# Halved column sums, attention operands split inside the projection, and modulation slots issued earlier, in a six-layer transformer kernel

## The chip, the cores and the metric

The kernel runs on one core of a Trainium2 chip, as one program and one launch. The metric is the device time of one execution in microseconds. TensorE (PE) multiplies matrices, VectorE (DVE), ScalarE (ACT) and GpSimd (POOL) work on rows of 128 partitions, and SyncE (SP) issues the DMA transfers.

## The reference

Two blocks run one after the other on 512 tokens of width 1024. The first has two hybrid layers; each mixes causal attention over selected keys, a gated linear attention and a pooling over token windows, and then applies a gated feed-forward network with a short convolution. The second has four layers on the same tokens laid out as a grid of 64 by 8, with 256 context tokens beside them; the kind of attention turns with the layer (0: grouped queries, 1: a neighbourhood window, 2: the difference of two maps, then 0 again).

```
h  = rms_norm(x, norm_g[i]) * (1 + sc) + sh        # sc, sh, gt = silu(c) @ ada_w[i] + ada_b[i]
hc = rms_norm(xc, norm_g[i]) * (1 + scc) + shc
u, z = split(h @ w_in);  uc, zc = split(hc @ w_in)
q, k = axial_rope(rms_norm(q, q_g)), axial_rope(rms_norm(k, k_g))       # kinds 0 and 2
o  = attention(q, [kc, k], [vc, v])                # kind 2: p0 - lam * p1, then a norm
lam = exp(sum(lq1 * lk1)) - exp(sum(lq2 * lk2)) + lambda_init
x  = x + gt * ((o * silu(z)) @ w_out)
```

`ada_w` is 1024 by 3072 for every one of the four layers; its products (the modulation) are worked out during the first block. Between the blocks x is normed once more (`final_norm_g`), and the first norm of the second block needs the sum of squares of every token again.

## The kernel before, in words

x lies in SBUF with the width on partitions: eight chunks k of 128 by the tokens (`M.xT[:, k, :]`). Every large product is made in float32 from two float32r parts: ACT rounds a weight slot of 128 by 1024 to its high part (L139, `split_high`), POOL subtracts to get the low part (L147, `split_low`), and PE multiplies high by high, high by low and low by high (L166). The two buffers of split slots are `M.head`, which stays for the whole program, and `WS`, which each stage takes anew; `M.W` is a ring of four slots loaded by DMA (L111).

The program is a sequence of stages (`stage`, L76 to L86). In a stage each engine has its own written order and waits on semaphores; at the end of each all engines meet. Nothing is scheduled by a planner. The stages that the change touches:

- `start`: x is loaded, ACT squares the chunks (L451), PE adds each chunk over the partitions with four matmuls against a column of ones (`column_sums`, L234), ACT takes the root (L241) and PE spreads it (L249). Then the first weight slot is split by ACT and POOL.
- `attention_by_keys` in the first block (16 works x of 128 queries; PE goes through scores L1104, transposes L1538, products L1553 and L1557). Beside it run the side programs of `MixedIn`: modulation products (L883, `slots`) whose weights go through the same ring `M.W`, their turning into columns (L898), and the two products of the pooled tokens (L1021), which DVE takes (L1043).
- `gated_linear_attention`: PE's order is written out by hand and holds `slots(a, b)` (24 weight slots of the modulation) and `columns(a, b)` between the steps of the attention. At the end DVE stores the modulation (L904), ACT and POOL split the first slot of the next stage into `M.head` (L154, L159), and SP waits for the slots loaded ahead (L115).
- `between_blocks`: DVE norms chunk k and turns its tokens into grid order (L314) into one of two buffers, ACT squares it (L286) and copies it back to `M.xT` (L287); PE adds 8 chunks of 512 tokens and 8 of 256 context tokens (L234).
- `values_projection` and `tiles_projection` in each second-block layer: 18 tiles t in a layer of kind 0, 24 in the others. For kind 0 tiles 0 to 7 are queries, 8 and 9 keys, 10 to 17 the gate z. Roots of the norms are taken at tile `z_tile + 2` (L2235, L2269), spread by PE (L2201) and applied by DVE (L2277).
- `first_rows`: a stage of its own, in which ACT rounds the first pair of heads (L1069, L1083), DVE and POOL make the low parts (L1072, L1086), and PE runs three idle products (`keep_running`, L175). For kind 1 it also loads the band of biases and adds the window (L1096), for kind 2 it works out lam (L2315 to L2329).
- `attention_by_keys` (kinds 0 and 1) or `difference_attention` (kind 2).

## Time and profile before

| | |
|---|---|
| time, median of 3 runs | 3480.87 us (3474.05 to 3481.51) |
| the profiled execution | 3467.25 us, span 3465.5 us |
| PE busy | 93% of the span |
| DVE, ACT, POOL busy | 43%, 39%, 33% |
| DMA | 260.00 MB, mean 75 GB/s |

The span is the time from the first to the last instruction in the profile; the time of the execution is 1.75 us more. Busy shares are averages over stages that have different limits. Where PE stands still its idle time is shown in square brackets behind the next instruction, with what ended it. PEclk is the clock that was granted to TensorE as a share of 2.4 GHz; 0.50 is 1.2 GHz. A matmul of float32 operands shows as two instructions in the trace.

### The profile page before, as it was taken

The numbers are of one execution on the slowest core, as the hardware profiler recorded it, in microseconds if no ns is written. First come the engines' busy times: TensorE is split into PE (matmuls) and PEld (weight loads), VectorE is DVE, ScalarE is ACT, GpSimd is POOL, SyncE is SP. The second block draws the span as 40 slices with busy tenths as digits, with TensorE's granted clock in tenths as the row PEclk, the third lists the DMA queues.
The fourth block names the chain that finished last, engine by engine and source line by source line (L and its number), as shares of the span: only waits on it lengthen the run. The fifth ranks groups of instructions, "written<-read, shape, count | busy, mean of one in ns | idle before, by whom it ended". The sixth has DMA issues, their size and how long they took to land. (4 is left out here: it accounts for less than half of the span.)

```text
span 3465.5 us, 52212 instructions
## 1 busy us (share of the span) xinstructions
PE 3223.5 (93%) x20824; PEld 2623.2 (76%) x20824; DVE 1503.8 (43%) x2673; ACT 1341.1 (39%) x2457; POOL 1143.7 (33%) x628
## 2 busy tenths in 40 slices
PE   7988999999989999989999999978999987799999
PEld 6856788777667887888787888767878766688687
DVE  4973443117744432132376310257323348733373
ACT  3352333223433332243366312257232236724463
POOL 3531444345414443424101322233234311225202
PEclk9999999999989999989999999999999999899999
DMA  4344222223442222212000111110112200013102
GB/s 142 113 168 168 81 96 92 88 86 119 166 175 79 93 96 88 97 59 89 26 2 20 55 56 61 55 41 14 49 62 85 80 20 1 1 50 105 47 2 74
DMA packets 80664, 260.00 MB, mean 75 GB/s; under 512 B 11808, under 2 KB 13600, under 8 KB 80416
## 3 DMA queue, kind: packets, MB, share of 16 engines
q1 hardware_dynamic: 80416, 256.58, 22.2%
q8 instruction: 169, 2.77, 0.3%
q14 instruction: 79, 0.65, 0.1%
HBM read 239.24 MB, written 2.10 MB: 70 GB/s over the span
## 5 line engine op out<-in xcount | busy, mean ns | idle before, releaser
L166 PE MATMUL ps<-hs,head 128*128 128x512 f32 x4176 | 882.3, 368 | 18.2 <-PEq L86 5.9
L166 PE MATMUL ps<-hs,WS 128*128 128x512 f32 x4176 | 869.3, 366 | 5.5 <-POOL WS L147 5.5
L166 PEld LDWEIGHTS ps<-hs,head 128*128 128x128 f32 x4176 | 717.1, 190 | 176.3 <-issue 19.4
L166 PEld LDWEIGHTS ps<-hs,WS 128*128 128x128 f32 x4176 | 714.2, 189 | 149.1 <-issue 9.1
L147 POOL TENSOR_TENSOR WS<-W,WS 128x1024 fp32r<-128x1024 f32 x168 | 408.7, 2433 | 637.9 <-ACT WS L139 637.9
L147 POOL TENSOR_TENSOR head<-W,head 128x1024 fp32r<-128x1024 f32 x165 | 399.1, 2419 | 653.0 <-ACT head L139 653.0
L139 ACT CAST WS<-W 128x1024 fp32r<-128x1024 f32 x168 | 175.9, 1047 | 360.0 <-PE ps L166 330.0
L1571 ACT ACTIVATE prob<-ps,low 128x768 f32<-128x768 f32 (+4 forms) x320 | 223.2, 699 | 192.2 <-DVE low L1643 189.9
L1104 PE MATMUL ps<-kk,qq 64*128 64x256 f32 (+3 forms) x2064 | 221.3, 342 | 71.9 <-ACT prob L1308 34.7
L1104 PEld LDWEIGHTS ps<-kk,qq 64*128 64x128 f32 x2064 | 163.8, 192 | 140.1 <-issue 73.9
L139 ACT CAST head<-W 128x1024 fp32r<-128x1024 f32 x165 | 172.8, 1047 | 214.6 <-PE ps L166 211.2
L1643 DVE TENSOR_REDUCE low<-ps 128x1 f32<-128x768 f32 (+4 forms) x320 | 216.5, 701 | 57.9 <-PE ps L1104 53.5
L1076 POOL TENSOR_TENSOR qq<-prj,qq 128x512 fp32r<-128x512 f32 (+1 forms) x52 | 53.1, 1022 | 455.8 <-ACT qq L1069 455.8
L1538 PE MATMUL ps<-const,prob 128*128 128x128 f32 x1312 | 185.0, 284 | 15.3 <-ACT probT L1579 13.0
L1975 DVE TENSOR_TENSOR glu<-cg,glu 128x512 fp32r<-128x512 f32 x44 | 81.1, 1843 | 270.7 <-ACT glu L1962 270.7
L1553 PE MATMUL ps<-probT,vtok 128*64 128x128 f32 x2624 | 179.2, 279 | 2.4 <-DVE prj L1627 2.4
L1538 PEld LDWEIGHTS ps<-const,prob 128*128 128x128 f32 x1312 | 143.7, 143 | 43.6 <-ACT prob L1571 22.5
L2239 ACT ACTIVATE prj<-ps,par 128x768 f32<-128x768 f32 (+1 forms) x52 | 45.2, 869 | 313.7 <-PE ps L166 313.7
L1553 PEld LDWEIGHTS ps<-probT,vtok 128*64 128x64 f32 x2624 | 140.6, 137 | 27.5 <-issue 27.3
L166 PE MATMUL ps<-glu,head 128*128 128x512 f32 x528 | 131.5, 406 | 11.7 <-PEq L86 11.7
L1579 ACT COPY probT<-ps 128x512 f32<-128x512 f32 (+3 forms) x272 | 139.4, 540 | 1.8 <-PE ps L1538 1.5
L2001 DVE TENSOR_TENSOR xT<-xT,ps 128x512 f32<-128x512 f32 x32 | 22.0, 687 | 269.3 <-PE ps L166 269.3
(283 smaller groups left out, 3924.7 us busy)
## 6 DMA issues: line engine op xcount, KB each, us to landing
W<-in_stream_dram SPq DMA_DIRECT2D x432, 512.0 KB, 3.5
swap<-prj SPq DMA_DIRECT2D x168, 64.0 KB, 2.4
band<-in_bias_band_dram SPq DMA_DIRECT2D x8, 512.0 KB, 3.4
prj<-prj SPq DMA_DIRECT2D x64, 64.0 KB, 3.0
xT<-in_x_dram SPq DMA_DIRECT2D x4, 512.0 KB, 8.4
W<-in_stream_dram SPq DMA_DIRECT2D x1, 2048.0 KB, 13.4
out_dram<-xT SPq DMA_DIRECT2D x8, 256.0 KB, 2.7
xT<-in_ctx_dram SPq DMA_DIRECT2D x1, 1024.0 KB, 6.0
```

What stands on the lines that cost most here:

```text
L139: nc.scalar.copy(WS[j % 2][:, 0, :], M.W[:, (pos + j) % RING, :]).then_inc(high, 1)
L147: nc.gpsimd.tensor_tensor(WS[j % 2][:, 1, :], M.W[:, (pos + j) % RING, :], WS[j % 2][:, 0, :], ALU.subtract).then_inc(split, 1)
L166: last = pe.matmul(out, a(i), b(j), start=start and n == 0, stop=stop and n == 2)
L1076: return self.nc.gpsimd.tensor_tensor(self.q_part(s, 1, cols), self.queries(t, cols), self.q_part(s, 0, cols), ALU.subtract)
L1104: last = pe.matmul(out(hd)[:, sc:sc + c], self.qq[half(hd), s, i, q0:q0 + P], self.kk[half(hd), s_keys, j, kc:kc + c], start=n == 0, stop= ...
L1538: last = pe.transpose(turn_at(y, hd, j), prob[:, (2 * y + hd) % 4, sc:sc + P], M.const[:, C_ID:C_ID + P])
L1553: pe.matmul(summed_at(hd), M.vtok[:, kb, v_col(p) + 64 * hd:v_col(p) + 64 * hd + 64], probT[:, (2 * y + hd) % 4, j, :], start=j == 0, stop ...
L1571: nc.scalar.activation(prob[:, u % 4, c0:c0 + n], W.scores(M, x, hd)[:, c0:c0 + n], ACT.Exp, bias=low[:, u:u + 1], accum_out=total[:, u:u ...
L1579: nc.scalar.copy(probT[:, u % 4, 0:n, :], M.ps[:, 4 + 2 * hd, 0:n * P].rearrange("p (x n) -> p x n", n=P)).then_inc(turn_copied, 1)
L1643: nc.vector.tensor_reduce(low[:, u:u + 1], W.scores(M, x, hd)[:, c0:c0 + n], AX_X, ALU.max, negate=True).then_inc(maxed, 1)
L1975: nc.vector.tensor_tensor(glu[:, 1, f - 2, :], g[:, f % 2, :], glu[:, 0, f - 2, :], ALU.subtract).then_inc(glu_split, 1)
L2239: nc.scalar.activation(M.prj[:, t, 0:n], flat(bank(t), n), ACT.Copy, scale=gain(t)).then_inc(evicted, 1)
```

## The change

It has these parts, named A to G below.

**A, between the blocks.** `turned` and `squares` hold all eight chunks. The copy back to `M.xT` is a DMA for each chunk, issued by SP, and no longer done by ACT. POOL adds the squares of each two chunks, and PE adds over the partitions only the four sums of pairs, and four of the context.

```diff
+                    sp.wait_ge(scaled, k + 1)
+                    sp.dma_start(M.xT[:, k, 0:S], turned[:, k, :]).then_inc(moved, 16)
                 sp.wait_ge(pars_loaded, 32)
+                sp.wait_ge(moved, 16 * KD)
...
-                    if k >= 2:
-                        act.wait_ge(added, k - 1)
-                    nc.scalar.activation(squares[:, k % 2, :], turned[:, k % 2, :], ACT.Square).then_inc(squared, 1)
-                    nc.scalar.copy(M.xT[:, k, 0:S], turned[:, k % 2, :]).then_inc(moved, 1)
...
+                    for c in range(2 * (k - 3), 2 * (k - 2)) if 3 <= k < 7 else ():
+                        nc.scalar.activation(ctx_squares[:, c, :], M.xT[:, c, S:N], ACT.Square
+                                             ).then_inc(ctx_squared, 1)
+                act.wait_ge(added, 1)
...
+                def pair(x, k, done, summed):
+                    pool.wait_ge(done, k + 2)
+                    nc.gpsimd.tensor_tensor(x[:, k, :], x[:, k, :], x[:, k + 1, :], ALU.add).then_inc(summed, 1)
+
+                for k in range(0, KD, 2):
+                    pair(squares, k, squared, paired)
+                    if k >= 4:
+                        pair(ctx_squares, 2 * k - 8, ctx_squared, ctx_paired)
+                        pair(ctx_squares, 2 * k - 6, ctx_squared, ctx_paired)
...
+                for i in range(KD // 2):
+                    pe.wait_ge(paired, i + 1)
+                    last = column_sums(pe, M, squares[:, 2 * i, :], 0, i == 0, i == KD // 2 - 1)
+                    for c in range(2 * (i - 2), 2 * (i - 1)) if i >= 2 else ():
+                        pe.wait_ge(ctx_paired, c + 1)
+                        last = column_sums(pe, M, ctx_squares[:, 2 * c, :], QT, c == 0, c == KD // 2 - 1)
+                last.then_inc(added, 1)
```

**B, the opening stage.** POOL adds chunks 4 and 5, and 6 and 7; PE adds six blocks where it added eight. A root of one column is taken ahead, so that the table of the square root is loaded earlier.

```diff
-                for k in range(KD):
+                for k in range(KD // 2):
                     pe.wait_ge(squared, k + 1)
-                    last = column_sums(pe, M, squares[:, k, :], 0, k == 0, k == KD - 1)
+                    column_sums(pe, M, squares[:, k, :], 0, k == 0, False)
+                for i, k in enumerate(range(KD // 2, KD, 2)):
+                    pe.wait_ge(paired, i + 1)
+                    last = column_sums(pe, M, squares[:, k, :], 0, False, k == KD - 2)
...
+                for k in range(KD // 2, KD, 2):
+                    pool.wait_ge(squared, k + 2)
+                    nc.gpsimd.tensor_tensor(squares[:, k, :], squares[:, k, :], squares[:, k + 1, :], ALU.add
+                                            ).then_inc(paired, 1)
...
                 nc.scalar.activation(M.cos[:], M.cos[:], ACT.Sin)
                 act.wait_ge(eps_set, 1)
+                nc.scalar.activation(M.rstd[:, QT:QT + 1], M.eps[:], ACT.Sqrt)
                 act.wait_ge(summed, 1)
                 column_root(nc, M, S).then_inc(rooted, 1)
```

**C, the causal attention.** The product of the pooled tokens is issued right behind the scores of its work, and DVE takes it in the same round; the fifth group of columns is turned at work 13. **E** (last lines): in the attention of the second block, kinds 0 and 1, PE runs four idle products behind the scores of works 0 and 1.

```diff
-    TURN_AT = {5: 0, 7: 1, 9: 2, 11: 3, 16: 4, 17: 5}
+    TURN_AT = {5: 0, 7: 1, 9: 2, 11: 3, 13: 4, 17: 5}
...
+    def mix(self, pe, x):
+
...
-        if x - 1 in self.MIX_AT:
-            i = self.MIX_AT[x - 1]
+        if x in self.MIX_AT:
+            i = self.MIX_AT[x]
             dve.wait_ge(self.mixed, i + 1)
...
+                        if x < 2 and not side:
+                            keep_running(pe, M, 4, 7)
+                    if side:
+                        side.mix(pe, x)
                     if 1 <= x <= X:
```

**D, the gated linear attention.** Each pair of slots stands one step earlier in PE's order, and so do the columns; the table of the square root is loaded one step earlier.

```diff
                 near_summed(2)
+                slots(8, 10)
                 near_summed(3)
-                slots(8, 10)
+                columns(1, 2)
                 pe.wait_ge(sums_copied, 1)
                 pe.wait_ge(gained_copied, 1)
                 turned_with_far(0)
+                slots(10, 12)
                 turned_with_far(1)
-                slots(10, 12)
                 turned_with_far(2)
+                slots(12, 14)
                 turned_with_far(3).then_inc(att_summed, 1)
-                slots(12, 14)
-                columns(1, 3)
+                slots(14, 16)
+                columns(2, 3)
                 pe.wait_ge(att_copied, QT)
                 pe.wait_ge(scanned, 1)
                 weighted(0)
-                slots(14, 16)
...
-                slots(16, 18)
+                slots(18, 20)
...
-                slots(18, 20)
+                slots(20, 22)
...
                 last.then_inc(square_sum, 1)
+                slots(22, 24)
                 columns(4, 5)
                 pe.wait_ge(inverted, 1)
...
-                slots(20, 24)
                 columns(5, 6)
...
+                nc.scalar.activation(rstd[:, 0, 0, 0:1], M.eps[:, 0:1], ACT.Sqrt)
                 rows(2)
-                nc.scalar.activation(rstd[:, 0, 0, 0:1], M.eps[:, 0:1], ACT.Sqrt)
```

**F, the operands of the first pair of heads.** In the layers of kind 0 (0 and 3) the stage `first_rows` is gone: its splits are done at tile `z_tile + 6` of `tiles_projection`, by ACT and POOL. **G**: lam is worked out in `tiles_projection` of layer 0. `first_rows` stays in the first block and for kinds 1 and 2, with 14 idle products for kind 1 and 5 for the others.

```diff
+    def lows(self, pool):
+
+        pool.wait_ge(self.queries_high, 1)
+        self.o.q_low_plain(0, 0, self.q_cols).then_inc(self.queries_low, 1)
+        pool.wait_ge(self.keys_high, 1)
+        self.o.k_low(0, 0, self.k_cols).then_inc(self.keys_low, 1)
 
...
+        rows_at = z_tile + 6
...
+            if map_weight:
+                map_weight.load(sp)
...
+                if rows_ahead and j == rows_at:
+                    rows_ahead.lows(pool)
...
+                if map_weight and t == 2:
+                    map_weight.exponential(act)
+                if rows_ahead and t == rows_at:
+                    act.wait_ge(normed, q_tiles + 2)
+                    rows_ahead.highs(act)
...
+            if map_weight:
+                map_weight.combine(dve)
...
+    def exponential(self, act):
+        act.wait_ge(self.lam_step, 2)
+        self.nc.scalar.activation(self.dots[:], self.dots[:], ACT.Exp).then_inc(self.exp_done, 1)
+
+    def combine(self, dve):
+        v, M = self.nc.vector, self.M
+        step = Chain(dve, self.lam_step)
+        dve.wait_ge(self.lam_loaded, 16)
+        step(v.tensor_tensor(self.prod[:], self.lam[:, :, 0, :], self.lam[:, :, 1, :], ALU.mult))
+        step(v.tensor_reduce(self.dots[:], self.prod[:], AX_X, ALU.add))
+        dve.wait_ge(self.exp_done, 1)
+        step(v.tensor_tensor(M.minus[:], self.dots[:, 1:2], self.dots[:, 0:1], ALU.subtract))
+        step(v.tensor_scalar(M.minus[:], M.minus[:], self.lambda_init, None, ALU.subtract))
+        v.tensor_scalar(M.sub_gain[:], self.par[:, R_SUB:R_SUB + 1], 1.0 - self.lambda_init, None, ALU.mult)
+
+
+def first_rows(nc, M, rows):
 
     band = rows.band
-    with ExitStack() as mem:
-        if lams is not None:
...
+        @block.tensor
+        def _(pe):
+            keep_running(pe, M, 14 if band else 5, 0)
...
+                if kind == 0:
...
+                ahead = kind == 0
+                new_operands = lambda: RowOperands(nc, M, operands_mem, n_out, N, 0, 1.0, k_tile, band)
+                if ahead:
+                    operands = new_operands()
+                    rows = FirstRows(operands, (0, S), (0, N))
...
+                with ExitStack() as project:
+                    last = KINDS.index(2)
+                    weight = MapWeight(nc, M, project, lams, LAMBDA_INIT[last], pars[:, last]) if i == 0 else None
+                    M.hs = sbuf(nc, project, "hs", [P, 2, KD, N], F32R)
...
+                                     lambda step: i + 1 < LAYERS and modulate(nc, M, pars, i + 1, step),
+                                     rows if ahead else None, weight)
...
+                if not ahead:
+                    operands = new_operands()
+                operands.add_second_buffers(operands_mem)
+                if not ahead:
+                    first_rows(nc, M, FirstRows(operands, (0, S), (0, N)))
```

The buffers `kk` and `qq` are now two each, the second of each taken after the projection. The split of weights into `M.head` and `WS` is as it was.

How PE's row changes between the blocks; `squares` and `ctx_squares` are the squared chunks, x counts matmuls, and four make one block of 512 tokens. Before:

```order
L234 MATMUL ps<-const,squares 128x1 x16
L234 MATMUL ps<-const,ctx_squares 128x1 x4
L234 MATMUL ps<-const,squares 128x1 x4
L234 MATMUL ps<-const,ctx_squares 128x1 x4
L234 MATMUL ps<-const,squares 128x1 x4
L234 MATMUL ps<-const,ctx_squares 128x1 x4
L234 MATMUL ps<-const,squares 128x1 x4
L234 MATMUL ps<-const,ctx_squares 128x1 x4
L234 MATMUL ps<-const,squares 128x1 x4
L249 MATMUL ps<-const,rstd 128x128 x6
```

After:

```order
L234 MATMUL ps<-const,squares 128x1 x12
L234 MATMUL ps<-const,ctx_squares 128x1 x4
L234 MATMUL ps<-const,squares 128x1 x4
L234 MATMUL ps<-const,ctx_squares 128x1 x4
L249 MATMUL ps<-const,rstd 128x128 x6
L83 UNCONDITIONAL_BRANCH
```

The sums of x fall from 32 matmuls to 16, those of the context from 16 to 8. 

PE's row at the end of the gated linear attention, from the last product of the attention (L1735) on; `ps<-W,cond` are slots, `ps<-const_61,row` columns, `sq_o` the sums of squares and `rstd_o` the spreading of the roots. Before:

```order
L1730 MATMUL ps<-att,vtok 64x128 x4
L1735 MATMUL ps<-q_state,after 64x32 x16
L898 MATMUL ps<-const_61,row 128x2 x4
L883 MATMUL ps<-W,cond 32x512 x4
L1780 MATMUL ps<-const_61,sq_o 128x2 x8
L898 MATMUL ps<-const_61,row 128x2 x4
L1788 MATMUL ps<-const,rstd_o 64x128 x16
L883 MATMUL ps<-W,cond 32x512 x8
L898 MATMUL ps<-const_61,row 128x2 x4
```

After (lines are those of the new file, L902 is L883 before, L917 is L898):

```order
L1773 MATMUL ps<-att,vtok 64x128 x4
L1778 MATMUL ps<-q_state,after 64x32 x16
L917 MATMUL ps<-const_61,row 128x2 x4
L902 MATMUL ps<-W,cond 32x512 x4
L1825 MATMUL ps<-const_61,sq_o 128x2 x8
L902 MATMUL ps<-W,cond 32x512 x4
L917 MATMUL ps<-const_61,row 128x2 x4
L1834 MATMUL ps<-const,rstd_o 64x128 x16
L917 MATMUL ps<-const_61,row 128x2 x4
```

The last eight slot products stood behind the spreading; now the last four stand ahead of it and ahead of the columns.

POOL's row at the end of `tiles_projection` in layer 3; `WS<-W` and `head<-W` are the low parts of weight slots, the last of them that of the next stage. Before:

```order
L147 TENSOR_TENSOR WS<-W,WS 128x1024
L147 TENSOR_TENSOR head<-W,head 128x1024
L147 TENSOR_TENSOR WS<-W,WS 128x1024
L147 TENSOR_TENSOR head<-W,head 128x1024
L83 UNCONDITIONAL_BRANCH
L85 ISA
L2303 UNCONDITIONAL_BRANCH
L1086 TENSOR_TENSOR kk<-prj,kk 128x768
```

After:

```order
L147 TENSOR_TENSOR WS<-W,WS 128x1024
L147 TENSOR_TENSOR head<-W,head 128x1024
L1108 TENSOR_TENSOR qq<-prj,qq 128x512
L1118 TENSOR_TENSOR kk<-prj,kk 128x768
L147 TENSOR_TENSOR WS<-W,WS 128x1024
L147 TENSOR_TENSOR head<-W,head 128x1024
```

The low parts of queries and keys now stand ahead of the low part of the slot of the last tile.

## Rows read from the trace of the kernel before

**Rows 1.** page, part 1: busy us and share of the span, instructions:

```profile
PE 3223.5 (93%) x20824; PEld 2623.2 (76%) x20824; DVE 1503.8 (43%) x2673; ACT 1341.1 (39%) x2457; POOL 1143.7 (33%) x628
```

**Rows 2.** timeline, opening stage: start us, us, engine line op xcount [idle before]:

```profile
9.47 13.81 PE L234 MATMUL ps<-const,squares 128*128 128x1 f32 x64 [9.47 <-DMA const<-in_const_dram]
...
23.37 1.28 ACT L241 ACT_TABLE_LOAD   x1 [5.93 <-PE ps L234]
24.67 0.26 ACT L241 ACTIVATE rstd<-ps,eps 128x4 f32<-128x4 f32 x1
```

**Rows 3.** windows, opening stage: us, busy by engine, PEclk, DMA share, GB/s:

```profile
19.00:20.00 1.00, 1.00 (x7) 1.00 (x6) 0.00 (x0) 0.00 (x0) 0.00 (x0) 1.00 0.03 5
```

**Rows 4.** timeline between the blocks:

```profile
1482.84 2.09 DVE L314 SCALAR_TENSOR_TENSOR turned<-xT,fg,ps 128x512 f32<-128x512 f32 x2 [2.30 <-PEq L86]
1484.63 5.58 PE L234 MATMUL ps<-const,squares 128*128 128x1 f32 x25 [2.79 <-ACT squares L286]
...
1488.86 0.42 ACT L292 ACTIVATE ctx_squares<-xT 128x256 f32<-128x256 f32 x1 [1.12 <-DMA xT<-in_ctx_dram]
...
1505.40 0.27 ACT L241 ACTIVATE rstd<-ps,eps 128x6 f32<-128x6 f32 x1 [5.01 <-PE ps L234]
```

**Rows 5.** timeline of the first causal attention, PE: its side product:

```profile
237.20 1.13 PE L1021 MATMUL ps<-w,par 128*128 128x512 f32 x2
```

**Rows 6.** timeline of the gated linear attention, first pass:

```profile
279.75 2.48 DVE L1878 TENSOR_TENSOR att<-ps,const 128x512 f32<-128x512 f32 x4 [13.23 <-PE ps L1721]
...
282.49 0.66 PE L1730 MATMUL ps<-att,vtok 128*64 128x128 f32 x8
...
296.76 3.39 PE L1788 MATMUL ps<-const,rstd_o 128*64 128x128 f32 x32
...
300.08 2.11 PE L883 MATMUL ps<-W,cond 128*32 128x512 f32 x16
...
304.21 0.21 DVE L904 COPY mods<-ps 128x48 f32 x1 [3.26 <-PE ps L898]
...
311.35 2.18 ACT L809 CAST hs<-hT 128x512 fp32r<-128x512 f32 x4 [5.30 <-PEq L86]
```

**Rows 7.** windows, the end of that stage:

```profile
308.00:309.00 1.00, 0.00 (x0) 0.00 (x0) 0.00 (x0) 0.00 (x0) 0.47 (x1) 0.50 0.81 332
```

**Rows 8.** timeline, the same end in the second pass:

```profile
1034.48 0.21 DVE L904 COPY mods<-ps 128x48 f32 x1 [3.50 <-PE ps L898]
...
1041.16 2.18 ACT L809 CAST hs<-hT 128x512 fp32r<-128x512 f32 x4 [4.84 <-PEq L86]
```

**Rows 9.** timeline, layer 0: end of the projection, operands, start of attention:

```profile
1699.66 0.81 ACT L2249 ACTIVATE prj<-ps 128x768 f32<-128x768 f32 x1 [6.65 <-PE ps L166]
...
1702.73 1.80 POOL L1086 TENSOR_TENSOR kk<-prj,kk 128x768 fp32r<-128x768 f32 x1 [7.24 <-DVEq L83]
...
1705.49 1.33 PE L1104 MATMUL ps<-kk,qq 64*128 64x512 f32 x12 [2.63 <-PEq L86]
...
1709.77 2.29 PE L1104 MATMUL ps<-kk,qq 64*128 64x512 f32 x12 [2.96 <-ACT prob L1571]
```

**Rows 10.** timeline, layer 3: the last tile of the projection:

```profile
3249.76 2.40 POOL L147 TENSOR_TENSOR WS<-W,WS 128x1024 fp32r<-128x1024 f32 x1 [4.73 <-ACT WS L139]
...
3253.55 5.64 PE L166 MATMUL ps<-hs,WS 128*128 128x512 f32 x24
```

**Rows 11.** timeline, layer 2: operands and map weight, start of attention:

```profile
2821.81 1.80 POOL L1086 TENSOR_TENSOR kk<-prj,kk 128x768 fp32r<-128x768 f32 x1 [7.24 <-ACT kk L1083]
...
2825.97 1.96 PE L1104 MATMUL ps<-kk,qq 64*128 64x512 f32 x12 [4.03 <-PEq L86]
```

**Rows 12.** timeline, layer 1: start of the banded attention:

```profile
2270.43 1.65 PE L1104 MATMUL ps<-kk,qq 64*128 64x256 f32 x12 [5.86 <-PEq L86]
```

**Rows 13.** timeline, layer 0: the reciprocals of the norms and their first use:

```profile
1641.97 4.96 DVE L2269 RECIPROCAL prj<-prj 128x512 f32<-128x512 f32 x2 [4.86 <-ACT prj L2235]
...
1649.22 1.52 PE L2201 MATMUL ps<-prj,const 32*64 32x512 f32 x16
```

165 lines of the change are left out of this document (73 added, 92 removed).

## The prediction

> **What bounds the kernel now.** I read the shares of busy time first: PE is busy for 93% of the span [rows 1], and none of its 20,824 large products is changed. What can be won or lost is PE's idle time and its side work at the joints of the stages, so I went through the timeline at each joint that the diff touches and asked what ended last there, and took from the windows whether the clock was granted and whether transfers were running. The reader is to see in each group one joint: the work that ends last before it, and the first instruction behind it. The sum is made against the profiled execution, 3467.25 us, which is 13.6 us (0.4%) under the median of the runs, 3480.87; the forecast is that median less the sum. Less than 0.2%, 7 us, can't be told from no change.
>
> **B, the opening stage.** PE runs its 64 column sums without a gap from 9.47 for 13.81 us, 0.216 each [rows 2]; 48 take 10.4, to 19.8, 3.4 us sooner. The table load of 1.28 at 23.37 stands on the path and moves under those sums; 4.7 in all. POOL's two sums of pairs (1.2 each, the 1.80 of 768 columns [rows 9] cut to 512) fit beside PE's first four chunks. Behind the root the first split needs the ring of weights; the transfers have ended by 19 to 20 us [rows 3], just in time. I take 4.3 (3 to 4.8).
>
> **A, between the blocks.** PE works from 1484.63 to the root at 1505.40 at 0.223 a sum (25 in 5.58) [rows 4], 96 instructions, and everything else waits for its turns. After, there are 48, 10.7 us, and the chain ahead counts: DVE's eight products need 8 x 1.05 from 1482.84, to 1491.2; ACT has the context at 1488.9 and its squares of 0.42 in between, so that the sixth square of x comes near 1491.5 (my estimate), POOL's pair 1.2 later, and PE has then 32 instructions left, 7.1 us: the root at 1499.9. Gain 5.5 (3 to 6.5). The copies by DMA are hidden: the first can be issued near 1484, the last near 1491, and their 2 MB take 6.3 us at the 332 GB/s of [rows 7], or 12.6 at half that rate, while the spreading behind the root ends only near 1503.
>
> **C, the causal attention.** The product of 1.13 [rows 5] goes ahead of the transposes, where DVE waits for it, then takes it, and only then masks the scores: the chain through DVE and ACT is 2 us later at work 14. At the end this product and the turned columns (about as long) are no longer on PE's path. I take a loss of 0.4 for each of two passes, -1.5 to +1: 0.8 in all.
>
> **D, the gated linear attention (two passes).** Before, the stage ends with transfers. The last products of slots start at 300.08, DVE's store of the modulation starts at 304.21, but the next stage starts at 311.35 [rows 6], and between 308 and 309 the DMA share is still 0.81 with PE at 0.50 [rows 7]. Now the last pair of slots stands ahead of the spreading. In PE's row a pair of slots costs 1.05 (16 instructions for two pairs in 2.11), and a group of columns about as much (my estimate). Two more of them than before stand ahead of the end of the scores and one group of columns more, so DVE's masking (279.75, 2.48) starts near 281.8 and the products with the values at 284.4 instead of 282.49. The later part of the row holds fewer slots; sums of squares end near 297.5, slots and columns take 2, the spreading runs from 299.5 (before 296.76) for 3.4, the last columns follow: the store is at 304.1, where it was. But the last loads are now issued near 298.5 and are there by 304, so the stage ends with the store, and 0.9 later, as other joints do (k_low ends at 1704.53, scores start at 1705.49 [rows 9]), the next begins: 305.2 against 311.35, 6.1. In the second pass the store is at 1034.48 and the next stage starts at 1041.16 [rows 8]; 5.5. I take 11 for both. Bounds: if the last landing still ends the stage, 2.5 each; if its restart at a granted clock also counts, 6.5 each.
>
> **F, operands inside the projection.** In layer 0 ACT's last eviction ends at 1700.47, the scores start at 1705.49 [rows 9]; without the stage between they start 0.9 after the eviction: 4.1. The splits' own place decides what is given back. ACT rounds queries and keys behind the high part of the last tile's slot; POOL then has both subtractions (1.2 and 1.8) ahead of the slot's low part (order of POOL above). In layer 3 that low part starts at 3249.76 and takes 2.40, and PE starts the last tile at 3253.55 [rows 10]. Now: 3249.76 + 0.6 (ACT's copy, 0.81 for 768 columns cut to 512) + 1.2 + 1.8 + 2.4 = 3255.8: PE stands still for 2.3 us. In layer 0 a tile is 1.5 times as wide, 8.5 us for 5.64, and the 2.8 more hide it, by half a microsecond. So 4.1 + 1.8 = 5.9. Bounds 4 (layer 0 pays too) to 8.2 (neither pays).
>
> **E, idle products in the attention.** Scores of work 0 take 1.33, those of work 1, the same, 2.29 [rows 9]: the clock fell to half in the 3 us of idling between. Four products (eight instructions of 256 columns, at most 0.235 each by the 24 in 5.64 of [rows 10]) fill 1.9 us of each gap. Works 0 to 2 gain 1 us of scores and some of the transposes, and lose where the filler stands ahead of the transposes of work 0: 0.8 each in layers 0 and 3. In layer 1 the 14 products fill the wait for the band, and the scores of 1.65 [rows 12] should take 0.9 at the full clock; 1.5. In all 3.1. Bounds: 0, if ACT and DVE pace these works whatever the clock, to 5; 3 are lost if the clock stays at half and the filler takes its double.
>
> **G, lam.** In layer 2 the low part of the keys ends at 2823.61, the scores start at 2825.97 and take 1.96 [rows 11]; without lam's chain they start 0.96 after POOL, 1.4 sooner, and at the full clock take 1.33: 2.0. In layer 0 the chain lies under tile 2; DVE is held until the exponential, but it would wait for POOL's half of the first rotation in any case. It costs a second table load: the root of the norms must load its own again, 1.28 us later. The reciprocals then end at 1648.2 instead of 1646.93, and PE first wants them at 1649.22 [rows 13]: hidden.
>
> What the skill says on this last point speaks against the change. The Trainium skill (ScalarE: Activation LUTs, What ACT_TABLE_LOAD costs) gives a switch of tables as the load of 1283 ns and a drain of about 1380 ns more. In this trace the root follows its table load at once: the load ends at 24.65, the root starts at 24.67 [rows 2]. By the rule the reciprocals would end at 1649.6 and PE would wait 0.4 us, and the sum would be 0.4 smaller; I stay with the trace.
>
> **The sum.** 4.3 + 5.5 - 0.8 + 11 + 5.9 + 3.1 + 2.0 = 31.0. 3480.87 - 31 = 3450.
>
> **The rivals.**
> - *The joints keep their price* (0.20). The stage of D still ends with its last landing (2.5 each, 6 less), A is paced by ACT and POOL (2 less), the fillers don't hold the clock (3 less), layer 0 pays for the splits too (2 less): gain 18, 3463. For it: rows 7 show that transfers ran at 332 GB/s to the end, so this stage lies near its transfer bound. Against it: 6 us lie between the last slots and the new end.
> - *More than forecast* (0.12). The clock stays up through all starts of attention and linear stages, and POOL's splits find room: gain 42, 3439. For it: windows at half clock behind each of these joints [rows 7]. Against it: the order of POOL is fixed.
> - *Slower: the ring of weights* (0.04). In D the slots stand a step nearer to the loads that feed them; each is issued only when the slot four before it has been multiplied, and PE works in order, so a slot that hasn't landed holds the attention steps behind it. 22 pairs in two passes: from 1.4 us for each pair the gain of 31 is gone, at 2 us the time is 3494. For it: transfers at 332 GB/s in this stage [rows 7]. Against it: the 1 MB of a pair takes 3.2 us at that rate, and with four slots in the ring another pair and at least two steps of the attention, 4 us by the distances in [rows 6], lie between a pair and its successor in the same buffers.
> - *Nothing to be seen* (0.04). What is won at the joints is given back behind them, since PE is 93% busy and the next wait is there already: 3478.
>
> The forecast's own case has 0.60, 3443 to 3458. Faster by over 0.2%: all of it, the first two rivals nearly whole, 0.91. Within 0.2%: 0.05. Slower: 0.04. The range, 3437 to 3464, takes in the first rival's time less its far end, the second's, and the bounds of the terms.
>
> **What would show it.** Right: 48 column sums for 64 at the start and the first root near 20 instead of 24.67; the root between the blocks about 5 us closer to its stage's start; in the gated linear attention the store of the modulation followed within 1 us by the next stage, and no DMA share in that gap; no stage between projection and attention in layers 0 and 3, and an idle time of PE of about 2.3 us before the last tile of layer 3, not of layer 0, ended by POOL's low part; a granted clock of 1.00 at the second scores of layers 0, 1 and 3. Wrong: PE waiting for DMA at a slot; the sixth square of x later than 1492; PEclk still at 0.50 behind the fillers; a gap at the spreading in layer 0.

## The result and the profile after

The changed kernel takes 3439.1 us (median of 3 runs, 3434.72 to 3444.5) against 3480.87 (3474.05 to 3481.51): ratio 0.9901, 95% interval 0.9877 to 0.9926. Forecast were 3450, range 3437 to 3464. In the profiled executions the time fell from 3467.25 to 3434.72 us, 32.5, against a sum of 31.0. So the two profiles agree with the sum. The medians of three fell by more, 41.8, and 3439.1 lies only 2 us inside the lower end of the range; the kernel before, run again below, shows why. Not all the terms behind the sum were right, and the rest of this section goes through them.

The page of the changed kernel, part 1 [rows 1]:

```profile
PE 3214.0 (94%) x20830; PEld 2611.4 (76%) x20830; DVE 1506.9 (44%) x2671; ACT 1340.8 (39%) x2452; POOL 1156.2 (34%) x640
```

PE has 9.5 us less to do and the span is 32.6 shorter. So 23 us of it are idle time of PE.

*B, the opening stage* [rows 2], timeline:

```profile
9.46 10.40 PE L234 MATMUL ps<-const,squares 128*128 128x1 f32 x48 [9.46 <-DMA const<-in_const_dram]
...
13.38 3.12 POOL L439 TENSOR_TENSOR squares<-squares 128x512 f32<-128x512 f32 x2 [12.08 <-ACT squares L469]
...
18.89 1.28 ACT L476 ACT_TABLE_LOAD   x1
...
20.30 0.25 ACT L241 ACTIVATE rstd<-ps,eps 128x4 f32<-128x4 f32 x1
...
24.88 1.62 PE L175 MATMUL ps<-const 128*128 128x256 f32 x3 [1.99 <-PEq L86]
```

The 48 sums end at 19.86, as worked out. The root is 0.5 later than that, since the table load is the new last step: the sines ahead of it wait for DVE (the first starts at 17.74), whose steps run while POOL adds its pairs. POOL takes 3.12 for two sums, where one took 1.27 between the blocks, and DVE's product of 512 columns beside them takes 1.65, where it took 0.69 before. The next stage starts at 24.88 instead of 29.27: 4.4 (forecast 4.3).

*A, between the blocks* [rows 4], timeline:

```profile
1470.51 8.15 DVE L325 SCALAR_TENSOR_TENSOR turned<-xT,fg,ps 128x512 f32<-128x512 f32 x8 [3.12 <-PEq L86]
...
1472.90 6.32 SPq L281 DMA_DIRECT2D xT<-turned  x8
...
1476.59 0.72 ACT L293 ACTIVATE ctx_squares<-xT 128x256 f32<-128x256 f32 x2 [1.32 <-DMA xT<-in_ctx_dram]
...
1487.39 0.27 ACT L241 ACTIVATE rstd<-ps,eps 128x6 f32<-128x6 f32 x1 [6.16 <-PE ps L234]
...
1491.63 0.67 PE L175 MATMUL ps<-const 128*128 128x256 f32 x2 [0.78 <-PEq L86]
```

From the start of DVE's first product to that of the root there are 16.88 us; before there were 22.56, a gain of 5.7 (forecast 5.5). The sixth square of x ends at 1478.96, 8.4 behind the start of DVE's first product (forecast 8.7): ACT waits for the context until 1476.59 and squares it between the chunks, as the working had it. The eight copies have landed by 1484.68, ahead of the root.

*D, the gated linear attention, first pass* [rows 6], timeline:

```profile
290.78 1.95 PE L1825 MATMUL ps<-const,sq_o 128*128 128x2 f32 x16
...
293.03 1.79 PE L902 MATMUL ps<-W,cond 128*32 128x512 f32 x8 [0.30 <-DMA W<-in_stream_dram]
...
294.75 1.87 PE L917 MATMUL ps<-const,row 128*128 128x2 f32 x8
...
296.55 3.67 PE L1834 MATMUL ps<-const,rstd_o 128*64 128x128 f32 x32
...
301.37 0.21 DVE L923 COPY mods<-ps 128x48 f32 x1 [0.34 <-PE ps L917]
...
302.45 1.14 ACT L828 CAST hs<-hT 128x512 fp32r<-128x512 f32 x2 [5.02 <-PEq L86]
```

The order of events is the forecast one: slots, columns, spreading, store, and 1.1 us behind the store's start the next stage, instead of 7.1; no transfer runs in that gap. The sums of squares end 46.2 us into the stage, as forecast. But the last pair of slots waits 0.30 for its load, one of the prediction's own signs of being wrong, and takes 1.79, the columns behind it 1.87, against 1.06 and 1.05. The granted clock is 0.56 from 293 to 295 and 0.50 from 295 to 300. So the store comes 1.9 us later in the stage than it did before, where the forecast had it in its old place. The stage takes 56.0 us against 60.2, a gain of 4.2 and not 6.1; the second pass takes 57.5 against 60.7, 3.1 and not 5.5.

*F, E, G*: layer 3 [rows 10], layer 0 [rows 9] and layer 2 [rows 11], PE:

```profile
3225.84 5.74 PE L166 MATMUL ps<-hs,WS 128*128 128x512 f32 x24 [2.05 <-POOL WS L147]
3233.12 1.31 PE L1136 MATMUL ps<-kk,qq 64*128 64x512 f32 x12 [1.54 <-PEq L86]
```
```profile
1683.07 1.31 PE L1136 MATMUL ps<-kk,qq 64*128 64x512 f32 x12 [1.76 <-PEq L86]
...
1687.34 1.31 PE L1136 MATMUL ps<-kk,qq 64*128 64x512 f32 x12 [1.03 <-ACT prob L1614]
```
```profile
2794.20 1.32 PE L1136 MATMUL ps<-kk,qq 64*128 64x512 f32 x12 [1.74 <-PEq L86]
```

Before layer 3's last tile PE waits 2.05 us for POOL's low part (forecast 2.3), in layer 0 not at all. The second scores of layers 0 and 3 take 1.31 and 1.30 (2.29 before). In layer 2 the first scores come 4.1 us after the stage's first product, not 5.6. G's second table load is hidden, as forecast: in layer 0 the reciprocals end at 1630.19, and PE starts the spreading at 1631.02 without having waited.

**Lengths of stretches.** To tell the terms from scatter I took the length of each stretch, between the same two instructions of PE, in every profile. This table is my arithmetic on the timelines of all runs below; "with it" are the kernels with that part in place (their number behind; those that alter the same stretch in another way are left out), "without" the kernel before (two profiles) and those in which the part is undone:

```
stretch                                 without the part          with it
opening stage                   (B)     29.27 29.26 29.31         24.80 to 25.00 (11)
input projection behind it      (B)     155.40 155.11 155.19      154.25 to 154.83, mean 154.5 (11)
between the blocks              (A)     32.30 32.57 33.20         26.43 to 27.45, mean 27.1 (11)
causal attention, both passes   (C)     66.5 to 71.1, mean 68.7   67.3 to 72.5, mean 69.9 (16)
  scores of work 13 to its end  (C)     18.1 18.1 19.6 19.6       19.3 or 19.4 (15), 20.4 (1)
                                        20.6 22.5
  last scores to its end        (C)     12.95 12.95 14.43 14.47   13.31 or 13.32 (15), 14.33 (1)
                                        15.48 17.39
gated linear attention          (D)     60.17 60.22 60.66 61.21   53.1 to 57.6, mean 55.8 (14)
                                        61.25 61.26
layer 0, projection + attention (F, E)  375.52 376.34             370.28 to 370.35 (8), 370.85 (1)
layer 3, projection             (F)     154.06 155.30 155.32      152.87 to 154.26, mean 153.7 (9)
layer 3, attention              (E)     148.67 148.67 148.70      147.87 to 147.91 (11)
layer 1, operands + attention   (E)     169.43 169.64 170.05      168.81 to 169.23 (10), 170.65 (1)
layer 2, operands + attention   (G)     218.97 221.60 220.85      218.41 to 220.66, mean 219.6 (9)
layer 2, projection (untouched)         316.45 314.67             308.68 to 314.25, mean 312.6 (10)
```

### The profile page after: what moved, and what is told of

Its sections match the earlier page's. It is cut to its first block and busy times, and to the rows that moved or that the text cites. A ratio compares the mean times of both kernels' runs of the same rounds, so it can differ in the third digit from the quotient of the medians.

```text
span 3432.9 us, 52180 instructions
## 1 busy us (share of the span) xinstructions
PE 3214.0 (94%) x20830; PEld 2611.4 (76%) x20830; DVE 1506.9 (44%) x2671; ACT 1340.8 (39%) x2452; POOL 1156.2 (34%) x640
## 5 line engine op out<-in xcount | busy, mean ns | idle before, releaser
L166 PEld LDWEIGHTS ps<-hs,head 128*128 128x128 f32 x4176 | 716.6, 190 | 175.2 <-issue 19.4
L1136 PE MATMUL ps<-kk,qq 64*128 64x256 f32 (+3 forms) x2064 | 219.3, 340 | 54.3 <-ACT prob L1347 33.9
L1108 POOL TENSOR_TENSOR qq<-prj,qq 128x512 fp32r<-128x512 f32 (+1 forms) x54 | 55.8, 1033 | 474.9 <-ACT qq L1101 474.9
L166 PE MATMUL ps<-glu,head 128*128 128x512 f32 x528 | 130.3, 403 | 11.6 <-PEq L86 11.6
```

The lines of the kernel that those rows point to most:

```text
L166: last = pe.matmul(out, a(i), b(j), start=start and n == 0, stop=stop and n == 2)
L1108: return self.nc.gpsimd.tensor_tensor(self.q_part(s, 1, cols), self.queries(t, cols), self.q_part(s, 0, cols), ALU.subtract)
L1136: last = pe.matmul(out(hd)[:, sc:sc + c], self.qq[s][half(hd), i, q0:q0 + P], self.kk[s_keys][half(hd), j, kc:kc + c], start=n == 0, stop= ...
```

## The experiments

**The same kernel again.** No edit.

> The changed kernel once more, to see what its time and its stretches do without any edit. Ratio to the kernel before 0.988 to 0.992. The sum of the terms was 31 us, but the comparison of the two profiles gives about 10 us less at the joints of the two attention stages of the first block and of layer 2, and about 10 us more in stretches that the change does not touch (layer 2's projections alone 3.9, the one of layer 1 1.5, in_projection 1.2, the linear stage behind layer 0 1.4). Theory 1, chance: those 10 us come from single waits of PE of 2 us for POOL's low parts, behind which the next tile takes 10.2 us instead of 8.65 because the clock has fallen; they fall at other tiles in every execution, so that here the same stretches differ from the first profile of the same kernel by 1.5 us or multiples, up or down, in at least three of them. Theory 2, they follow from the change (other starting times of loads): then each stretch is within 0.3 us of the first profile of the changed kernel.

3438.18 us (3429.43 to 3444.16, 6 runs), ratio 0.989 (0.9871 to 0.9909). The same place of the causal attention in the first profile, and in this one (timeline, PE):

```profile
219.00 1.07 PE L902 MATMUL ps<-W,cond 128*32 128x512 f32 x8
...
221.85 1.02 PE L917 MATMUL ps<-const,row 128*128 128x2 f32 x8
...
224.63 0.55 PE L1136 MATMUL ps<-kk,qq 64*128 64x128 f32 x6
```
```profile
220.95 1.07 PE L902 MATMUL ps<-W,cond 128*32 128x512 f32 x8 [1.85 <-issue]
...
224.42 1.71 PE L917 MATMUL ps<-const,row 128*128 128x2 f32 x8
...
227.53 1.93 PE L902 MATMUL ps<-W,cond 128*32 128x512 f32 x8
229.39 0.55 PE L1136 MATMUL ps<-kk,qq 64*128 64x128 f32 x6
```

Up to the pair of slots at 219 the two agree within 0.2 us. Here the pair comes 1.9 us later. PE is idle for most of the stretch from 219 to 221; the granted clock is then 0.87 from 221 to 223 and 0.50 from 223 to 229, and the products take up to twice their time (the turned columns 1.71 for 1.02). At the next scores of 0.55 this execution is at 229.39, the other at 224.63: 4.8 us apart, about 4.6 of them for a wait of 1.85. Theory 1 holds for the first block: its causal attention differs by 4 us between executions of one kernel. It is wrong in its detail for layers 1 to 3, where the two profiles differ by up to 1.2 in a stretch, not by multiples of 1.5; theory 2, within 0.3, is wrong too.

**The kernel before again.** No edit.

> The kernel before once more, for its stretches; the ratio is 1. In its first profile the projection of layer 1 (from the end of layer 0's linear stage) took 307.03 us and that of layer 2 316.45, against 303.3 to 305.4 and 311.5 to 313.7 in five profiles of the changed kernel and its variants, though no edit touches them. Theory 1, the clock's falls behind single waits of PE land on other tiles from one execution to the next: here these two are 304 to 307 and 312 to 316, at least one of them 1.5 us or more from its first value. Theory 2, they follow from the change: 307.0 and 316.4 again, within 0.3. The causal attention has been 67 or 71.5 us long whatever the kernel; here too one or the other, with a late slot and a clock at half behind it where it is 71.5.

3474.38 us (3469.95 to 3482.93, 10 runs), ratio 1.0007 (0.9994 to 1.0019). The projection of layer 1 took 304.26 (307.03 in the first profile), that of layer 2 314.67 (316.45): theory 1, at least half of what "untouched" stretches seemed to give was scatter. About 2 to 3 us in layer 2's projection may be real; no part of the change explains them, and the kernels below that undo one part don't single one out. The causal attention took 69.88 and 68.09. The 11 runs of the kernel before beside the first four kernels have a median of 3474.1, the other groups 3474.23, 3473.79 and 3472.51: the median that the forecast started from, 3480.87 of three runs, was 7 us too high.

**Without D.** The order of before in PE's and ACT's programs:

```
-                slots(22, 24)          # ahead of the spreading
 ...
+                slots(20, 24)          # behind it
                 columns(5, 6)
```

> Only D is undone: in the gated linear attention slots and groups of columns stand where they stood before, and the table of the square root is loaded behind the third row. As the prediction had it, 6.1 + 5.5 = 11.6 us more than the changed kernel, and the stage from its first POOL instruction to the next stage again near 60.1 us in the first pass, with PE idle for about 7 us behind the store. By the comparison of the profiles (55.98 against 60.14 in the first pass) 4.2 and about 3 to 4, 7 to 8 us in all. Rival, the transfers are only moved: less than 3 us in all.

3447.01 us (3445.47 to 3450.83), ratio 0.9921 (0.9905 to 0.9937), 8.8 more than the changed kernel, between the two forecasts of 11.6 and 7 to 8. Both passes took 61.26 and 61.25 us; timeline of the end of the first:

```profile
300.82 2.24 PE L902 MATMUL ps<-W,cond 128*32 128x512 f32 x16
...
305.07 0.21 DVE L923 COPY mods<-ps 128x48 f32 x1 [3.38 <-PE ps L917]
...
311.94 1.66 ACT L828 CAST hs<-hT 128x512 fp32r<-128x512 f32 x3 [5.04 <-PEq L86]
```
```profile
305.00:307.00 2.00, 0.00 (x0) 0.00 (x0) 0.21 (x1) 1.04 (x1) 0.02 (x1) 1.00 1.02 356
```

The store is at 305.07, the next stage 6.9 us later, and the DMA engines are busy until about 309. The trace also has the landing of every load. The last load of this stage, in the kernel before and in the changed one (source L111; issued, and us to landing; the second window holds the last two loads, and the later one has the 5.0):

```profile
L111 SPq DMA_DIRECT2D W<-in_stream_dram x1: 332/332/332, 303.1 to 303.1; - x1
...
DMA to landing us min/median/max: 7.1/7.1/7.1
```
```profile
L111 SPq DMA_DIRECT2D W<-in_stream_dram x2: 332/332/333, 295.0 to 295.5; - x2
...
DMA to landing us min/median/max: 4.3/4.6/5.0
```

The last landing is thus at 310.26 before and at 300.48 after. I compared it with the next stage's first product in every profile. In all eight passes without D that product comes 1.11 or 1.12 us behind the last landing, and 6.4 to 7.0 behind the end of the store. In 12 of the 16 passes with D and all bytes it comes 0.90 or 0.91 behind the end of the store, with every load landed by then; in the other four it is again 1.1 behind the last landing, but only 1.0 to 2.4 behind the store. So the last landing ended the stage before, and D mostly moves it out of the way. Over all profiles D gives 60.8 - 55.8 = 5.0 us a pass.

**One pair of D behind the spreading again.**

```
                 last.then_inc(square_sum, 1)
-                slots(22, 24)
                 columns(4, 5)
 ...
                     last.then_inc(spread, 1)
+                slots(22, 24)
                 columns(5, 6)
```

> D with one step of it undone: the last pair of slots stands behind the spreading, the others and the groups of columns as in the changed kernel. It tells which part of D's 5 us a pass (60.2 to 61.3 without it, 53.1 to 57.5 with it, from the stage's first POOL instruction to the next stage's first product) comes from the end. If the last loads are what ended the stage before, that is half or more of it: the stage is 2.5 to 4 us longer than in the changed kernel (58 to 60) and the store is followed by an idle PE of 2 to 4 us. Rival, the order ahead of it is what counts, because the loads of the last pair are issued once the pair four slots before is multiplied: within 1 us of the changed kernel, or shorter, because the last pair no longer runs at half clock ahead of the spreading.

3447.0 us (3439.3 to 3451.59), ratio 0.9924 (0.9902 to 0.9946): the total can't tell this kernel from the one without D. The stage took 57.27 and 58.51 us, 1.5 and 2.7 above the mean with D, in part short of the 2.5 to 4 expected; timeline, first pass:

```profile
293.87 3.30 PE L1833 MATMUL ps<-const,rstd_o 128*64 128x128 f32 x32
...
300.46 0.21 DVE L923 COPY mods<-ps 128x48 f32 x1 [2.50 <-PE ps L917]
...
304.42 2.18 ACT L828 CAST hs<-hT 128x512 fp32r<-128x512 f32 x4 [4.28 <-PEq L86]
```

The spreading stands ahead of the pair, and the store comes 1.6 us sooner in the stage than in the changed kernel; then PE has nothing to do for 4.1 us. In both passes the next stage starts 1.1 behind the last landing. With one pair left behind, the stage ends 3.8 us after its store, with two pairs 6.4 to 7.0. Those are the loads that the pairs release: the ring's next slots, which belong to the next stage, and which this stage ends with. Theory and rival were both true in part: the end decides, and the order ahead of it gives a little back.

**Without C.** The mix product behind the transposes and taken a round later, the columns at work 16:

```
-    TURN_AT = {5: 0, 7: 1, 9: 2, 11: 3, 13: 4, 17: 5}
+    TURN_AT = {5: 0, 7: 1, 9: 2, 11: 3, 16: 4, 17: 5}
```

> Only C is undone: the product of the mixed part behind the transposes, taken a round later, and the turned columns at work 16. If C costs what the profiles show (0.8 us in the first pass between the start of the causal attention and the start of the gated linear attention), this is 0.8 to 1.6 us faster than the changed kernel, about 0.03%, and the stage is 0.8 shorter. As predicted (0.4 a pass): 0.8 in all. Rival, C gains what was seen as lost elsewhere: 1 to 3 us slower.

3442.65 us (3432.08 to 3446.09), ratio 0.991 (0.9894 to 0.9925): not the 0.8 to 1.6 us faster that was expected, and within the interval of the changed kernel. From the scores of the last work to the next stage the profiles with C have 13.3 us every time but one; without it the best is 12.95, the others 14.4 to 17.4. PE then waits 1.8 us for ACT with nothing in between, and in four of the six passes the mix product behind it took 1.7 to 2.1 us (PE here, first pass; the mix product took 1.13 before):

```profile
237.39 0.63 PE L1577 MATMUL ps<-const,prob 128*128 128x128 f32 x4 [1.81 <-ACT probT L1618]
...
242.82 2.08 PE L1041 MATMUL ps<-w,par 128*128 128x512 f32 x2
```

That stretch leaves out the columns that C moves ahead of the last scores. All of C lies in the stretch from the scores of work 13 to the end: 18.1 us undisturbed without it and 19.3 with it, so that C costs 1.2 a pass where nothing goes wrong, not 0.4. By the means, 19.8 and 19.4, it is paid back. The stage as a whole is 1.2 longer with C by the means (69.9 against 68.7); that difference arises ahead of work 13, where C has changed nothing.

**Without A, B and G.** Functions of before for the first two, the map weight's chain back in layer 2's stage of the operands.

> A, B and G are undone together, since they lie in three separate places: the opening stage, the stage between the blocks, and lam in layer 2 instead of layer 0. Opening stage: the first product behind it 4.4 us later than in the changed kernel. Between the blocks: stage 5.7 us longer. G: by the prediction layer 2 from the last low part of the keys to the end of its attention is 2.0 us longer; by the comparison of the profiles its start is 1.4 later, but the end of the attention not (0 to 0.4), because a work there is paced by the chain of ACT and DVE. Sum by the prediction 11.8 us slower than the changed kernel, by the comparison 10.4.

3452.45 us (3449.14 to 3455.01), ratio 0.9936 (0.992 to 0.9951): 14.3 more than the changed kernel, where 11.8 and 10.4 were expected. Opening stage 4.4 longer, the input projection behind it 0.7 longer, the stage between the blocks 6.1. Layer 2's attention takes 220.85, 0.2 above what the kernels with G scatter over (218.41 to 220.66). The first scores come 1.2 us later than with G. By the scores of the fourth work the kernels without G are at 20.8 to 21.1 us in the stage and seven of the nine with it at 18.8 or 18.9 (the ones without F and without E at 19.7 and 19.3): the 2.0 that was forecast. Behind that the executions of one kernel drift apart by 1 to 3 us, and what is left at the end is 0.8 by the means, which can't be told from 2.0 or from nothing.

**Without F.**

```
-                ahead = kind == 0
+                ahead = False
```

> Only F is undone: the operands of the first pair of layers 0 and 3 are made in a stage of their own again. By the prediction 4.1 us longer in layer 0 and 1.8 in layer 3 from the start of the projection to the first scores, 5.9 in all, 0.17%; PE stands still before the last tile of neither layer (2.05 us in layer 3 in the changed kernel). Rival, the overlap is paid for elsewhere: less than 3 us in all.

3448.97 us (3446.18 to 3451.4), ratio 0.9925 (0.9905 to 0.9946). Layer 0 took 374.51 us to the end of its attention (370.3 with F): 4.2. Layer 3's projection 155.32, against a mean of 153.7: 1.6. That is 5.8, forecast 5.9; the other 5 by which this kernel is slower than the changed one lie in stretches that it doesn't touch.

**Without E.** No idle products behind the scores, 3 instead of 14 and 5 ahead.

> Only E is undone: no idle products behind the first two works' scores, 3 instead of 14 (layer 1) and 5 (layer 2) in the stage of the operands. By the prediction 0.8 us longer in the attention of layers 0 and 3 and 1.5 in layer 1; by the profiles 0.8, 0.8 and 1.0 (170.05 against 169.0 from the mark of the operands' stage to that of the linear stage); second scores at 2.2 instead of 1.31. Rival, the idle products have nothing to do with it and the attention is paced by ACT and DVE: lengths within 0.2 of the changed kernel.

3436.79 us (3435.58 to 3438.64), ratio 0.9892 (0.9872 to 0.9912): the total can't tell it. The stretches can, since these two vary by 0.1 us: 148.70 against 147.89 in layer 3, and 0.84 more in layer 0, where the second scores are at half clock again:

```profile
1687.54 2.29 PE L1136 MATMUL ps<-kk,qq 64*128 64x512 f32 x12 [2.96 <-ACT prob L1612]
```

In layer 1 it is 169.43 against a mean of 169.0 with E, 0.4; the two profiles of the kernel before have 170.05 and 169.64. That is 0.4 to 1.0, not 1.5. With E the first scores there did take 0.98 instead of 1.65, and the granted clock from 2244 to 2252 is 1.00, against 0.50 here. By the fourth scores the stage with E is 0.8 to 1.4 us ahead, and a part of that is gone by its end; PE waits for POOL's low part of the keys in every case, 5.3 us in all with E, 4.1 here and 5.0 in the kernel before.

**Three more edits, in three places of the changed kernel.**

```
-                if rows_ahead and j == rows_at:
+                if rows_ahead and j == rows_at + 1:
 ...
-                t = j - (2 if shared else 3)
-                if rope and 0 <= t < z_tile:
+                for t in (j - 3,) if not shared or j <= z_tile else (j - 3, j - 2):
+                    if not (rope and 0 <= t < z_tile):
+                        continue
 ...
+                        if x < 2:
+                            keep_running(pe, M, 4, 7)       # layer 2's attention
```

> Three edits in three separate places of the changed kernel, each read from its own stretch. (1) POOL makes the low parts of the first pair one slot later in layers 0 and 3, behind the low part of the last tile's slot: PE's 2.05 us of waiting before layer 3's last tile goes, layer 3 to its first scores is 2 us shorter; rival, the low parts then end the joint and the scores start later by as much. (2) In layer 2's projection POOL multiplies by the cosines one tile later, the last two together. Theory: a low part there waits for a chain of low part 2.4, exchange by DMA 4.4 to 6.1 and product 1.8, about 9 to 10.6 us against a tile's 8.65, so that PE stands still for 5.4 us in six waits and the clock falls behind the longest; with a tile's slack these go, and the stretch of 311.5 to 314.3 takes 306 to 309. Rival, they come back where two products stand together at the end: no change. (3) Four idle products behind the scores of works 0 and 1 in layer 2's attention: by the measured 0.8 of layers 0 and 3 it would be 0.8 shorter (218.4 to 220.8 before); rival, this attention is paced by the chain of ACT and DVE and the fillers change nothing or cost up to 1 us. Sum 4 to 8 us faster than the changed kernel.

3425.67 us (3420.34 to 3429.31), ratio 0.9865 (0.9846 to 0.9885): the fastest of all, 12.5 below the changed kernel, where 4 to 8 were expected. (1) Layer 3's last tiles, PE, in the changed kernel's second profile and here:

```profile
3231.81 7.33 PE L166 MATMUL ps<-hs,WS 128*128 128x512 f32 x24 [2.05 <-POOL WS L147]
```
```profile
3211.66 5.64 PE L166 MATMUL ps<-hs,WS 128*128 128x512 f32 x24
```

A wait of 2.05, and a tile of 7.33 instead of 5.64 behind it: 3.7 us for a stall that I had priced at 2.3. The tile took 7.33 to 7.39 in every profile with F and the wait but the first, which had it in 5.74. In that one the granted clock stayed at 1.00 behind the wait, in the second it was 0.78 and then 0.69. Without the wait the projection of layer 3 takes 150.39 us, 3.3 less than the mean, and the scores start as soon behind it as before, so that the rival fell. (2) Waits of PE in layer 2's projection, in the changed kernel and here (engine, line, waited for: us in total, times, longest); the kernel before had 4.9 and 2.8:

```profile
PE ps L166 <- POOL head L147: 4.2, 3, 2.4
...
PE ps L166 <- POOL WS L147: 2.2, 3, 1.2
```
```profile
PE ps L175 <- PEq L86: 2.6, 2, 1.8
PE ps L166 <- DVE hs L366: 2.2, 1, 2.2
PE ps L1136 <- PEq L86: 1.7, 1, 1.7
PE ps L166 <- PEq L86: 1.5, 1, 1.5
PE ps L249 <- DVE rstd L227: 0.6, 1, 0.6
```

The waits for POOL are gone and the stretch takes 304.57 us, 8 less than the mean of the others. In the changed kernel the waits come to 6.4, and PE's own work is 2.7 us longer (300.30 busy, 297.62 here). The kernel without E happened to have 3.5 us of these waits, and its stretch lies in between, at 308.68. DVE is busy for 68.3 us here and was for 97.7: its sums of 512 columns take 0.69 each, where all but one took 2.8 beside POOL's low parts. The chain stands in both kernels and no part of the change touches it. (3) Layer 2's attention took 217.19, and 215.94 in the last run, against a mean of 219.6: by the third scores it is 0.9 ahead, as in layers 0 and 3, and by the fourth 1.9.

**A quarter of the loads' bytes, with D and without.** 20 of the 24 loads of the modulation's slots in each of the four stages bring 128 KB instead of 512; the last four, which are the next stage's slots, stay whole. The products run over old data.

```
+        c = n if j + RING < count else SLOT
+        sp.dma_start(M.W[:, (pos + j) % RING, 0:c],
```

> The changed kernel with a quarter of the bytes in 20 of the 24 loads of the modulation's slots in the two attention stages of the first block (the rest of each slot keeps old data, so this part of the computation is left out). It takes the transfers away as a bound and leaves every instruction. Theory: the late slots of the causal attention go (length 66.5 to 68 in both passes instead of 67.3 to 72.5), and the gated linear attention loses the waits for slots but not more, since the last slots now stand ahead of the spreading: 53 to 55 us a pass instead of a mean of 55.8. Rival, the scatter of both stages is the clock's alone and has nothing to do with slots: lengths still scatter by 4 us.

> As the kernel with a quarter of the bytes, and D undone in it; the same part is left out. If what D gains (5 us a pass, 60.8 against 55.8) is the time of transfers that ended the stage, nothing of it is left: the gated linear attention takes 53 to 55.5 us with either order. Rival, D gains by PE's order itself: 2 us a pass or more remain.

3429.66 us, ratio 0.988 (0.986 to 0.99), with D; 3447.62, 0.9925 (0.9909 to 0.9942), without. With D the causal attention takes 66.71 and 66.70, the gated linear attention 52.46 and 52.28, less than the 53 to 55 expected, and PE waits for a slot in neither. In the second kernel, whose causal attention is the same, it doesn't wait for a slot either, but the first pass takes 69.75 us and the second 66.71: in the first the granted clock is 0.50 from 182 to 186.5, the first pair of slots takes 1.93 for 1.07, and 2.2 of the 3 us are lost by the fourth work. So the slots' loads make part of the scatter, and a part is left without them; the rival holds in part. The second expectation's theory fell: without D the stage still takes 61.45 and 59.49 us. The end of it with the two orders (timeline; first with D):

```profile
296.45 0.21 DVE L925 COPY mods<-ps 128x48 f32 x1 [0.35 <-PE ps L919]
...
298.82 1.66 ACT L830 CAST hs<-hT 128x512 fp32r<-128x512 f32 x3 [4.58 <-PEq L86]
```
```profile
299.03 2.38 PE L904 MATMUL ps<-W,cond 128*32 128x512 f32 x16
...
303.42 0.21 DVE L925 COPY mods<-ps 128x48 f32 x1 [3.52 <-PE ps L919]
...
310.35 2.18 ACT L830 CAST hs<-hT 128x512 fp32r<-128x512 f32 x4 [5.09 <-PEq L86]
```

Without D it ends with four whole loads, 2 MB, issued behind the last slots, whatever the others carry: the last lands at 309.26, the next stage starts 1.1 later. With D, too, the last landing (297.74) ends this shorter stage, 2.2 behind the store. D puts most of that tail beside PE's work and gains 8 us a pass here (60.5 against 52.4). With all the bytes it gains 5. Waits for slots are a part of what is given back: the 14 passes with D in the table have 19 of them in this stage, of 0.3 to 1.6 us, the six without D one, of 0.4. They are not all of it: the last kernel below has none there and takes 54.3 and 55.7 us, at a mean granted clock of 0.88 and 0.84, against 0.93 with a quarter of the bytes. Why the clock differs is not shown.

**Single slots.** On top of the three edits, in the causal attention one slot behind the transposes and one at the end of a round:

```
+                    if side:
+                        side.product(pe, 2 * x)
 ...
-                        side.products(pe, x)
+                        side.product(pe, 2 * x + 1)
```

> The three edits of the run before (3425.7, ratio 0.9865), and in the causal attention the two slots of a round apart: one behind the transposes, one at the end, each waiting for its own load, so that loads are issued one at a time and not two together. Theory: the causal attention has 66.7 us with a quarter of the bytes and 67.3 to 72.5 with all of them, because a pair of slots comes late in the 3 us round at work 10 and the clock falls behind it; with single loads the queue is even, the late slot is rare and both passes take 66.5 to 68.5 (70.2 was the mean), 2 to 3 us less a pass: 3420 to 3423. Rival 1, the transfers' rate decides and not how they are issued: 67 to 72.5 again, and 3426. Rival 2, the slot in the middle is wanted 2 us sooner than before and stands ahead of the products with the values, so that late slots are more frequent: 71 to 73 in both passes, 3430.

3434.62 us (3429.15 to 3438.62), ratio 0.9886 (0.9866 to 0.9907): 9 slower than with the three edits alone. The causal attention takes 77.2 and 75.9 us. But PE hardly waits for slots any more (0.2 us for DMA in the first pass, nothing in the second); the price is another (PE, a pair in the kernel of three edits, then single slots):

```profile
198.26 1.07 PE L902 MATMUL ps<-W,cond 128*32 128x512 f32 x8
```
```profile
199.43 1.05 PE L900 MATMUL ps<-W,cond 128*32 128x512 f32 x4
...
201.33 1.05 PE L900 MATMUL ps<-W,cond 128*32 128x512 f32 x4
```

The eight instructions of a pair take 1.07, the four of one slot 1.05. Each slot has two strips of 32 partitions of the sums, and the two slots of a pair have different ones; in the trace the four strips' instructions start within 0.02 us of each other and run side by side. Apart, each slot pays a full microsecond, 12 x 1.03 = 12.4 us a pass, of which 10.5 and 9.2 show against the 66.7 of the kernel without slots' waits. The late slots did go, and it didn't pay. None of the three outcomes I had written down has this mechanism; the second rival, 71 to 73 and 3430, comes nearest and is too small.

## Why the prediction was right, and where it was not

- *B* 4.3 forecast, 4.4 measured, and 0.7 more in the projection behind it, where the granted clock over 40 us is 0.96 for 0.91 (from 31 us behind the stage's start). That POOL's sums and DVE's steps slow each other was not in its working; it cost the root about 0.5.
- *A* 5.5 forecast, 5.6 measured as stretch. The sixth square came 8.4 us behind DVE's first product, paced by the context's landing; the working had 8.7 the same way.
- *C* -0.4 a pass forecast. Undisturbed it is -1.2, three times that; by the means of the stretch it is +0.4, since without it the clock falls there more often. The price of the chain through DVE and ACT was put too low, and the fall of the clock that C avoids was not in the working.
- *D* 11 forecast, 10.0 measured (5.0 a pass). The first two profiles had 7.3 in both passes. The mechanism is right: the last landing ended the stage, as its distance of 1.1 us from the next stage shows in every pass without D, and the pair left behind. The term that was off is what PE's row costs ahead of the spreading: "slots and columns take 2" took 3.8 (1.79 + 1.87 and a wait of 0.3), at half clock.
- *F* 5.9 forecast, 5.8 measured. But "PE stands still for 2.3 us" is 3.7 in most executions, with the clock's part; layer 3 still gains since its whole stage of operands goes.
- *E* 3.1 forecast, 2.0 to 2.6 measured: 0.8 and 0.8 as worked out, layer 1 0.4 to 1.0 instead of 1.5. The scores there do run at full clock and the fourth ones come 0.8 to 1.4 sooner, but not all of it reaches the end; the step that failed is that every us gained on the scores shortens that attention.
- *G* 2.0 forecast. The first scores come 1.2 to 1.4 sooner and the fourth work's 2.0, as worked out; at the end 0.8 is left by the means, with an uncertainty as large. PE waits 34 us there for ACT over 29 waits, but it waited 35 before, so this doesn't show where the gain went, and that stays open.
- *The table load*: in the trace after, the root (20.30) follows its table load (18.89 to 20.17) and a small root at once. The drain of 1.4 us that the Trainium skill (ScalarE: Activation LUTs, What ACT_TABLE_LOAD costs) adds to a load is not to be seen here either, nor in layer 0, where G's load ends at 1624.13 and the root starts at 1624.14; staying with the trace was right.

Together the terms come to 30 to 32 us, 31 forecast, with two that were too high (D, E) and others that were too low (B, C); that the sum is so near is in part luck. The changed kernel's six later runs give 3474.1 - 3438.2 = 35.9 by the medians, 31.6 at the near end of the interval. What is missing, up to 6 us, I can place only in part (layer 2's projection, 2 to 3). The forecast of 3450 was above the result mostly because its base, three runs, was 7 us above what 40 runs of the same kernel gave later; from 3474 the same sum gives 3443.

Of the rivals, "joints keep their price" (3463) fell with rows of D; "more than forecast" (3439) has the right time by the wrong way: the clock did not stay up through the starts of linear stages. The rival of the slower side, the ring of weights, is real but small. In the gated linear attention, where it was expected, late pairs came with D: 19 in 14 passes, against one in six passes without D, of 0.3 to 1.6 us and not 1.4 for each pair. Late pairs in the causal attention, up to 2.1 us, stood in both kernels; one of 1.85 cost about 4.6 in all.
